# Behind the experts, a full tile first and the eight sample rows second, in a one-core decoder step

## What is computed

```python
# experts: 32 of them, two per row, weights cw
for e in range(N_EXPERTS):
    h_e = silu(x @ w_gate[e]) * (x @ w_up[e])
    y = y + cw[:, e:e + 1] * (h_e @ w_down[e])
h = h + y
# gate on the per-layer embedding
gate = sigmoid(rmsnorm(h, g_ple) @ w_ple_gate)        # 1024 x 1024
h = h + (p @ w_ple_proj) * gate
return rmsnorm(h, g_final)
```

## Time and profile before

| | |
|---|---|
| median of 3 runs | 906.82 us (903.97 to 911.71) |
| profiled execution | 905.17 us |
| its span, first to last instruction | 903.3 us |
| TensorE, VectorE, ScalarE, GpSimd busy | 82%, 29%, 23%, 21% |
| mean granted TensorE clock | 0.97 |

### The profile page before, as it was taken

How to read it: one execution, slowest core, us unless ns; L and a number is a source line. 1 busy time by engine, 2 the same in 40 slices (tenths; PEclk the granted TensorE clock), 3 DMA queues, 4 the chain that set the end, 5 groups by cost and what they waited for, 6 DMA issues and landing times.

```text
span 903.3 us, 10684 instructions
## 1 busy us (share of the span) xinstructions
PE 738.3 (82%) x4173; PEld 433.8 (48%) x4173; DVE 258.0 (29%) x405; ACT 205.6 (23%) x310; POOL 193.9 (21%) x205
## 2 busy tenths in 40 slices
PE   4999998999689878999877777777777777773796
PEld 3999875999658632333222222222222222221585
DVE  5421446489931282000000000000000000003775
ACT  7333411324201222111101010101001010103566
POOL 1463362234801102122111112121211112110000
PEclk9999989999989999999999999999999999997798
DMA  9722141002441377999999999999999999994301
GB/s 364 291 96 77 67 175 47 1 2 81 177 174 50 119 285 295 401 424 431 423 424 428 424 426 427 427 424 427 427 427 426 426 426 427 424 427 187 135 26 70
DMA packets 27761, 253.32 MB, mean 280 GB/s; under 512 B 5834, under 2 KB 6386, under 8 KB 13512
## 3 DMA queue, kind: packets, MB, share of 16 engines
q1 hardware_dynamic: 19200, 234.50, 62.5%
q0 software_dynamic: 7776, 16.90, 4.9%
q10 hardware_dynamic: 752, 1.45, 0.4%
HBM read 246.06 MB, written 15.04 MB: 289 GB/s over the span
## 4 chain that ended last, share of the span: by engine, by line
PE 47%; DMA 39%; DVE 8%; ACT 3%; issue 2%; SPq 1%; DVEq 0%; ACTq 0%; POOLq 0%
DMA arena<-in_w_exp 35%; PE ps L1510 17%; PE ps L1721 10%; PE ps L1631 5%; PE ps L1833 4%; PE ps L1737 2%; DMA arena<-in_w_ple_gate 2%; PE ps L1518 1%; PE ps L1592 1%; PE ps L1582 1%; PE ps L1564 1%; PE ps L1647 1%; PE ps L1498 1%; DVE wo_lo L1131 1%; SPq L483 1%
## 5 line engine op out<-in xcount | busy, mean ns | idle before, releaser
L1721 PE MATMUL ps<-arena,region_u 128*64 128x512 f32 x992 | 224.9, 597 | 60.7 <-DMA arena<-in_w_exp 60.0
L1721 PEld LDWEIGHTS ps<-arena,region_u 128*64 128x64 f32 x992 | 69.5, 136 | 214.4 <-issue 138.0
L1361 DVE TENSOR_TENSOR region_u<-region_u,ps 128x256 f32<-128x256 f32 x32 | 13.5, 421 | 430.2 <-ACT region_u L873 430.2
L1510 PE MATMUL ps<-u_hi,w_hi 128*128 128x260 f32 x448 | 130.2, 291 | 0.2 <-DVE u_lo L1173 0.2
L1510 PE MATMUL ps<-u_lo,w_hi 128*128 128x260 f32 x448 | 128.2, 286 | 0.0
L1510 PE MATMUL ps<-u_hi,w_lo 128*128 128x260 f32 x448 | 128.2, 286 | 0.0
L1737 PE MATMUL ps<-arena,region_u 128*64 128x512 f32 x512 | 116.9, 598 | 9.5 <-DMA arena<-in_w_exp 4.5
L653 POOL DMA_INDIRECT y_rows<-region_v,scol x32 | 33.8, 1057 | 378.5 <-ACT region_v L877 378.5
L552 POOL TENSOR_TENSOR w_lo<-arena,w_hi 128x1024 fp32r<-128x1024 f32 x28 | 68.7, 2456 | 125.5 <-ACT w_hi L726 125.5
L1510 PEld LDWEIGHTS ps<-u_hi,w_hi 128*128 128x128 f32 x448 | 86.2, 192 | 2.3 <-issue 1.7
L1510 PEld LDWEIGHTS ps<-u_lo,w_hi 128*128 128x128 f32 x448 | 86.1, 192 | 0.1
(11 more groups left out here) (299 smaller groups left out, 848.9 us busy)
## 6 DMA issues: line engine op xcount, KB each, us to landing
arena<-in_w_exp SPq DMA_DIRECT2D x94, 2048.0 KB, 24.6
arena<-in_w_in SPq DMA_DIRECT2D x6, 2048.0 KB, 12.0
arena<-in_w_o SPq DMA_DIRECT2D x2, 2048.0 KB, 8.5
arena<-in_w_ple_gate SPq DMA_DIRECT2D x2, 2048.0 KB, 23.6
xh<-in_x SPq DMA_DIRECT2D x4, 512.0 KB, 5.5
arena<-in_w_in SPq DMA_DIRECT2D x4, 512.0 KB, 8.9
region_m<-in_state_ret POOLq DMA_DIRECT2D x8, 256.0 KB, 6.6
out_ret_s<-region_m POOLq DMA_DIRECT2D x8, 256.0 KB, 2.6
```

The source lines that it names most:

```text
L1510: last = mm(halves(out)[:, half, :], w[:, k, :], u[:, k, cols], start=(k == 0 and s == 0), stop=(k == KD - 1 and s == 2))
L1721: last = mm(ps[side * 64:side * 64 + 64, 2 + b, :], xv[:, k // 4, k % 4, :], rows(k % 4 * 2 + side), start=(k == 0), stop=(k == KD - 1))
```

## The change

1. **Order of tiles.** `TAIL_TILES` begins with full tile 0, and the eight sample rows (`FEW`) stand second. The jobs become `u0 pa0 u1 pb0 pg1 u2 pa2 u3 pb2 pa3 u4 pb3 pa4 pb4 pc4`, where place 1 is the eight rows.
2. **y in two transfers.** For the first tile the two halves of `y` (one for each chosen expert) are loaded by two DMAs with a semaphore each, and `combine(0, 0)` waits for the first alone.
3. **Eviction ahead of the high part.** `evac_out` of the last expert stands ahead of all four `gate_high_part`.
4. **VectorE's low pieces.** The third and the fourth piece stand behind the split of the first tile.
5. **One root behind the last sigmoid.** The square root of the last but one tile (`final_sqrt`) moves behind the last sigmoid `pc`, where it takes the place of a square root that only loaded the table, and `final_norm` of that tile moves behind the last `gated`.

```diff
-TAIL_TILES = [NT - 1] + list(range(NT - 1))
-TAIL = [("u", 0), ("u", 1), ("pg", 0)]
-for _n in range(1, NT):
-    TAIL += [("pa", _n)] + ([("u", _n + 1)] if _n + 1 < NT else []) + [("pb", _n)]
+TAIL_TILES = [0, NT - 1] + list(range(1, NT - 1))
+FEW = TAIL_TILES.index(NT - 1)
+
+def first_kind(n):
+    return "pg" if n == FEW else "pa"
+
+TAIL = [("u", 0)]
+for _n in range(NT):
+    TAIL.append((first_kind(_n), _n))
+    if _n + 1 < NT:
+        TAIL.append(("u", _n + 1))
+    if _n != FEW:
+        TAIL.append(("pb", _n))
 TAIL.append(("pc", NT - 1))
...
-                sp.dma_start(y_buf[n % 2][0:m, :], y_tok[r0:r0 + m, :]).then_inc(y_loaded[n % 2], 16)
+                if n == 0:
+                    sp.dma_start(y_buf[0][:, 0:D], y_tok[r0:r0 + m, 0:D]).then_inc(y_first, 16)
+                    sp.dma_start(y_buf[0][:, D:2 * D], y_tok[r0:r0 + m, D:2 * D]).then_inc(y_loaded[0], 16)
+                else:
+                    sp.dma_start(y_buf[n % 2][0:m, :], y_tok[r0:r0 + m, :]).then_inc(y_loaded[n % 2], 16)
...
-                    if last and b == 1:
-                        gate_high_part(0)
...
-            for q in range(1, 4):
+            for q in range(4):
                 gate_high_part(q)
...
-            for n in range(NT):
-                if n + 1 < NT:
-                    high_rows(n + 1)
-                sigmoid("pa" if n else "pg", n)
+            for n in range(NT - 1):
+                high_rows(n + 1)
+                sigmoid(first_kind(n), n)
                 if n:
                     final_root(n - 1)
-                if n + 1 < NT:
-                    gate_root(n + 1)
-                if n:
+                gate_root(n + 1)
+                if n != FEW:
                     sigmoid("pb", n)
+            sigmoid("pa", NT - 1)
+            final_square(NT - 2)
+            sigmoid("pb", NT - 1)
             last_square(0, "pa").then_inc(part_square, 1)
             sigmoid("pc", NT - 1)
-            link(nc.scalar.activation(stats[:, 40:41], eps, ACT.Sqrt))
+            final_sqrt(NT - 2)
             last_square(1, "pb").then_inc(part_square, 1)
             last_root()
...
-                if n == 0:
-                    gate_low_part(2)
-                if more and n != 1:
+                if more and n:
                     combine(n + 1, 0)
                 dve.wait_ge(u3_hi_ready, n + 1)
                 V.tensor_tensor(u3_lo[n % 2][:, 0:width], u3T[n % 2][:, 0:width], u3_hi[n % 2][:, 0:width],
                                 ALU.subtract).then_inc(dve_tail, 1)
-                if n == 1:
+                if n == 0:
+                    gate_low_part(2)
                     gate_low_part(3)
                     combine(n + 1, 0)
...
             gated("pc", NT - 1)
+            final_norm(NT - 2)
             last_norm()
```

More of the change, by code:

```diff
@@ L384, in build @@
         y_loaded = [sem(f"y_loaded{i}") for i in range(2)]
+        y_first = sem("y_first")
         hy_done, hy_root, hy_rstd = sem("hy_done"), sem("hy_root"), sem("hy_rstd")
@@ L939, in gate_root, with final_square @@
                                      scale=1.0 / D, bias=eps[0:m, :]).then_inc(hy_root, 1)
-            def final_root(n):
+            def final_square(n):
                 t = TAIL_TILES[n]
@@ L946, in final_root, with final_sqrt @@
                                           accum_out=stats[0:m, t:t + 1]))
+            def final_sqrt(n):
+                t = TAIL_TILES[n]
+                m = TILES[t][1]
                 nc.scalar.activation(stats[0:m, 5 + t:6 + t], stats[0:m, t:t + 1], ACT.Sqrt, scale=1.0 / D,
                                      bias=eps[0:m, :]).then_inc(f_root, 1)
+            def final_root(n):
+                final_square(n)
+                final_sqrt(n)
             def last_square(part, kind):
@@ L1385, in combine @@
                 yb, h = y_buf[n % 2], xh[0:m, t, :]
-                if k == 0:
+                if n == 0 and k == 0:
+                    dve.wait_ge(y_first, 16)
+                elif n == 0 or k == 0:
                     dve.wait_ge(y_loaded[n % 2], 16 * (n // 2 + 1))
@@ L1472, in _ @@
             gate_rstd(0)
[L1473 to L1476, removed]
+            for n in range(NT - 1):
+                split_rows(n + 1)
+                gated(first_kind(n), n)
                 if n:
                     final_norm(n - 1)
-                if n + 1 < NT:
-                    gate_rstd(n + 1)
-                if n:
+                gate_rstd(n + 1)
+                if n != FEW:
                     gated("pb", n)
+            gated("pa", NT - 1)
+            gated("pb", NT - 1)
             dve.wait_ge(part_square, 2)
@@ L1825, in _ @@
                         for k in range(KD):
-                            if turn == 1 and k % 4 == 0:
+                            if turn == 0 and k % 4 == 0:
                                 pe.wait_ge(gate_lo_ready, 2 * half + k // 4 + 1)
```

## The result

| | before | after |
|---|---|---|
| median of 20 runs | 906.33 us (903.97 to 914.34) | 913.05 us (910.92 to 921.43) |
| profiled execution, span | 903.3 us | 910.4 us |
| last `down` ends at | 821.15 us | 822.05 us |
| **tail**: from there to the end of the span | 82.15 us | 88.4 us |

The ratio is 1.0074 (95% interval 1.0050 to 1.0097): the change costs 6.7 us. That is less than 1%, but clear of the noise, and it lies 0.55 us above the range that was forecast (904.0 to 912.5). Those differ by 6.2 us here.

A forecast was written before the change was run, and what follows sets the result against it. Until 842.34 us transfers, eviction and combining were taken to bound the tail, then TensorE, then a closing chain. TensorE's end +0.7 and the closing chain +0.7 put 906.82 + 1.4 = 908.2 us, range 904.0 to 912.5.

The forecast's parts named there:

- three signs of being wrong: On TensorE: first gate matmul later than 842, no wait behind u2, or waits elsewhere, above all ahead of u1.
- The seam, "I take 825.9": Last expert to first tile: scatter issued at 822.67 lands at 825.9, first gate matmul at 838.0, head start 4.3 us.
- The half clock on `pa0`: First full product: loses 1.8 us at half clock while the eight-row product regains 2.1, cancelling within 0.3 us.
- The new wait: TensorE behind u2: nothing covers that tile's split, so it costs +3.8 us, bounds 3.5 and 4.0.
- The clock in that wait: TensorE's idling behind u2 may halve the clock, losing 0 to 1.7 us; 1.0 was taken.
- The end: Behind the last matmul: nothing gained on ScalarE, 0.4 us added on VectorE and 0.3 by the store, +0.7 us.
- The covers: pa0 on TensorE covers the low pieces and eight-row combines with 0.2 us to spare; at full clock, a 1.6 us wait.
- the scatter is caught in the stream: Rival at the seam: the earlier scatter meets gate weights, takes 8.1 us, lands at 830.8; sum 913.1 us, chance 0.10.

The follow-up runs named there:

- e2_root: Kernel before with only the last but one tile's root behind the last sigmoid and its normalization behind the last gated part: 907.96 us, ratio 1.0028.
- e12_scatter_free: Kernel before with the early eviction, plus the second 2 MB gate-weight load moved behind the first two loads of y: 914.25 us (one run).
- e3_cover: Changed kernel with the eight-row product placed behind u2 on TensorE, so that it covers that tile's split: 907.26 us, ratio 1.0009.
- e4_fill: Changed kernel with four added, unread float32 matmuls in TensorE's wait behind u2: 911.25 us, ratio 1.0028.
- e8_warm_new: Changed kernel with added unread float32 matmuls, 13 ahead of the first transposes and 4 ahead of pa0: 911.78 us, ratio 1.0075.
- e5_one_y: Changed kernel with the first tile's y loaded in one 1 MB transfer instead of two: 918.54 us, ratio 1.0127.

## Why the prediction was wrong

The forecast was +1.4 us on the median; +6.7 came out. The mechanisms were the ones named, but four sizes were off, all in the same direction. None of the three signs of being wrong appeared (the first gate matmul came at 840.2 on the old time scale, TensorE waited behind `u2`, and not ahead of `u1`); what failed was the last matmul, 5.3 us later relative to `down` where it should have been within 2. By the terms of the sum, measured on the tail:

- **The seam, "I take 825.9"** (head start 4.3 us). This is the step that failed most. The eviction and the issue of the scatter were right within 0.1 us. The landing was taken as 3.2 us behind the issue; it was 4.5. I had subtracted 0.9 us for the long GpSimd instruction, but e2_root and e12_scatter_free land in 3.3 us with an instruction of 1.9 and of 1.0 us, so that subtraction was not borne out, and the load still in flight added 1.2 on top. The second half of `y` landed 5.6 us behind the first issue, forecast 5.05. The rule of the Trainium skill's page "DMA: Bandwidth & Descriptors" (section on queues, rings and completion order) that the engines take turns between queues, which I weighed as making the sum 0.8 us smaller, was no help. The trace shows the longer landing while 15% of the engines' time was taken. First product at 19.0 us behind `down`, forecast 16.8. Missed by **2.2 us**.
- **The half clock on `pa0`**, "the two cancel within 0.3 us". It lasted 5.8 us of the work, not 3.6. I had named 5.6 us as a bound; it makes the term +0.7 (2.8 less 2.1), 1.0 above what I took. The 2.1 was also misread: 262.4 and 265.7 in the earlier trace rows are the first and the last start, so the product in the head took 3.3 + 0.38 = 3.7 us, and the loss that goes away was about 1.7. Measured: `pa0` loses 2.7 and the other product gets back 1.8, +0.9 in place of -0.3. Missed by **1.2 us**.
- **The new wait**: forecast +3.8, measured 4.0, and e3_cover removes it with the clock's part for 5.0. Right, in place and in size. It is the largest single cause.
- **The clock in that wait**: forecast 1.0 of 0 to 1.7, measured 1.4 (e4_fill) and up to 2.7 (e8_warm_new, e5_one_y). The section of the Trainium skill that I weighed, in "TensorE: Matmul & The Clock Gate" on HAM oscillation, would have counted it in full, 1.7. The traces agree with it: the clock fell in each of the three kernels that left this wait empty. Here it was the better guide. Missed by **0.4 us**, and the upper bound was too low.
- **The end**: forecast +0.7, measured 0.9 to 1.0 (e2_root): 0.4 for VectorE, as forecast, and 0.5 behind the issue of the last stores, forecast 0.3. ScalarE's saved root and table loads are worth nothing, as argued.
- **The covers**: `u1` did not wait in the changed kernel, and would have by 1.15 us with `pa0` at full clock (forecast 1.6). Right.

With 0.2 each from the wait and the end and 0.1 from the eight rows' transposes that is 4.3 us of the 4.8 by which the tails missed the forecast; the other 0.5 are the small change named above. By the medians the miss is 5.3 us, and the interval of the ratio alone reaches from 4.5 to 8.8. The rival "the scatter is caught in the stream" gave nearly the measured time, 913.1 us, but by a mechanism that did not occur at that size: it needed a landing of 8.1 us, and 4.5 were measured. I do not count it as right; the agreement is luck. The range was too narrow, since it took the several open terms as if at most one of them would go to its bad end; they all hang on transfers and on the clock, and all went there.

## What to carry to other kernels

When an order of tiles is changed on an engine that sets the end, look at each hand-over that needs a trip through other engines, and ask which work of another tile stands in it: here one placement of the eight-row product was worth 5.0 us, and the order that looked better had two such holes. Before an order is changed to bring a tile forward, look at what held it: here it was one 2.3 us piece in VectorE's queue, which could be moved alone. Count a TensorE wait of some 4 us together with the half clock behind it, as one price.

## What was unexpected of the hardware

- A wait of 4.0 us on TensorE, between dense stretches, brought the clock down to half in each of the three kernels that had it with nothing in it (after, e5_one_y, e8_warm_new), and cost 1.4, 2.7 and 2.6 us in the product behind it (5.7 us at full clock). With 3.6 us of added float32 matmuls in it the clock stayed.
- A scatter of 128 rows landed in 3.3 us with nothing in flight (e12_scatter_free), in 3.3 to 3.4 us where it went out as the last load ended (before, e2_root), in 4.5 us with that load in flight (DMA share 0.15), and in 8.1 us, the median, in the middle of the full stream. GpSimd's own instruction took 1.9 us in the second case and 1.0 in the first, without a difference in the landing.
- 1 MB of `y` took 5.7 us from issue to landing right behind the scatter, and 4.7 us further back.
